# A transformer layer with a product-key expert stage: a wider dense part of V in rounded halves, and sixteen dots on TensorE

## The chip, the cores and the metric

The kernel runs on one core of one Trainium2 chip. The metric is the device time of one execution in microseconds; a core's engines are TensorE (PE), VectorE (DVE), ScalarE (ACT), GpSimd (POOL) and SyncE (SP), which run their own instruction streams and meet through semaphores. Sixteen DMA engines move data between HBM and the on-chip memory (SBUF).

## The reference

One layer on 256 tokens of width 2048: a mixer (two kinds of attention) and then an expert stage. Only the expert stage is touched:

```python
def chunk(xc):                                   # 128 tokens
    qc = (xc @ w_query).reshape(C, 8, 2, 128)
    s = einsum('chpd,hpnd->chpn', qc, sub_keys)  # 2 x 128 keys a head
    top_s, top_i = lax.top_k(s, 16)
    ...                                          # 16 of the 256 sums, an expert of 16384 each
    g = softmax(best_s)
    act = gelu(einsum('chkd,cd->chk', expert_u[expert_idx], xc))
    return einsum('chk,chkd->cd', g * act, expert_v[expert_idx])
x = x + out
```

Each token picks 8 x 16 = 128 experts, so each of the two tiles of 128 tokens has 128 picks: for pick m a row of `expert_u` (2048 floats) is fetched for each token and its dot product with the token is taken, and the row of `expert_v` is added with the weight that follows from it.

## The kernel before

The work of the two tiles is numbered as 256 picks, m = 0 to 255; 16 picks are a "head" here, heads 0 to 7 belong to tile 0 and 8 to 15 to tile 1. Partition p holds token p of a tile.

**U stage.** POOL issues one indirect DMA per pick (line 691, 128 rows of 8 KB, 1 MiB) into one of eight places (`ring`; six from pick `U_WIDE` on). DVE takes the dot in one pass over the row (`pick_dot_of`, line 1549) and raises `dotted`; between the dots it does the top-k work of the next head (`head_part`, ten parts in the first ten picks of a head), and the last part gives `pick_row`, without which POOL can't issue the next head's gathers. From m = 112 (`V_FROM`) on POOL puts a gather of V between every four of U (`v_gather`, line 671); V rows are only `V_ROW` = 1152 wide. The first 36 of them (`V_BESIDE`) are added by PE: ACT makes a diagonal matrix of the weights (line 917) and PE multiplies it with the rows (`pick_add`, line 2095, true fp32).

**Dense part.** The other `V_DENSE` = 896 columns of V aren't gathered. For each token a 128 x 128 matrix of its weights over all 16384 experts is built from two one-hot matrices (`group`, line 2118, four tokens each), and moved by ACT into `dense_w[t][b, a, token]` (`group_out`, line 961). Then PE multiplies it, block a of 128 expert rows by block, with the whole table: `dense(a)`, line 2127, 128 blocks, both tiles, fp32. The blocks are loaded by SP into four places (line 598), each as soon as the block four before it has been used.

**Seam.** Tile 0's weights are built beside the U stage; tile 1's, which need the last dot, in the stage between it and the first dense block, called the seam. `SEAM` is the order of the V rows there: DVE adds one after two of every three groups of four tokens (line 1597), PE one after every second group; 37 rows in all, into seven places. Per group DVE makes two one-hot blocks (line 1582), ACT scales four matrices and moves the result, PE multiplies four pairs.

**Tail.** PE runs the 128 dense blocks; DVE adds the 183 rows of V that are left, POOL gathers them through the seven places in order. The last row's add is cut in two, and the outputs leave by DMA.

Of the kernel before, what the change touches and what calls it, by code (L numbers as in the profile page):

```python
# [14 lines left out]
P = 128  # L15
# [118 lines left out]
U_WIDE = 108  # L134
# [3 lines left out]
V_ROW = 1152  # L138
V_DENSE = D - V_ROW
V_FROM, V_BESIDE = 112, 36  # L140
# [9 lines left out]
SEAM = sorted([(i, "dve", i) for i in range(GROUPS) if i % 3] + [(i + 2, "pe", i) for i in range(GROUPS) if i % 2])  # L150
# [3 lines left out]
DENSE_AT = (4 * 512, 6 * 512)  # L154

# [17 lines left out]

def v_place(k):

    return k % V_FIRST_PLACES if k < V_BESIDE else (k - V_BESIDE) % V_PLACES
# [12 lines left out]
def v_until(m):  # L189

    return max(0, m - V_FROM + 1) // 4
# [43 lines left out]
def layer(nc, x, norm1_g, w_in, cmp_pe, cmp_k_w1, cmp_k_w2, cmp_v_w1, cmp_v_w2, q_norm_g, k_norm_g,  # L235
          rel_bias_table, sb_out_g, nsa_out_g, w_out, norm2_g, peer_w_query, peer_sub_keys,
          peer_expert_u, peer_expert_v, onehot, out):
    with ExitStack() as ctx:
# [147 lines left out]
        assert A_XN <= at_big[0] - DENSE_PLACES * V_DENSE and at_big[0] <= A_X1T  # L386
        hot0 = ring_rest.rearrange("p (s j n) -> p s j n", s=2, j=GROUP_TOKENS)
# [26 lines left out]
        query_used = sem("query_used")  # L414

# [195 lines left out]
        def _(pool):  # L611
# [63 lines left out]
            for m in range(PICKS):  # L675
                if m in (0, 8):
                    pool.wait_ge(sem("first_rows"), m // 8 + 1)
                elif m % TOPK == 0:
                    pool.wait_ge(head_step, (m // TOPK + 1) * HEAD_OPS)
                if m == 0:  # L680
                    pool.wait_ge(split_free, SP_END + SPLIT)
                if m == EARLY - 1:
                    pool.wait_ge(sem("rows_gained"), TT * W_CHUNKS)
                if m == TOPK - 4:
                    power(8, rstd[:, 1:2])
                f = before_in_place(m)
                if f >= 0:
                    pool.wait_ge(dotted, f + 1)
# [11 lines left out]
        def _(act):  # L700
# [233 lines left out]
            def hot_first(i):  # L934

                for j in range(GROUP_TOKENS):
# [4 lines left out]
                    act.activation(v, iota[:, :], ACT.Square, bias=picks_t[:, 1, token:token + 1], scale=-1.0).then_inc(sem("hot_squared"), 1)  # L941
                    act.wait_ge(sem("hot_squared"), token + 1)
# [15 lines left out]
            def group_out(t, i):  # L958

                act.wait_ge(token_made, t * P + (i + 1) * GROUP_TOKENS)  # L960
                act.activation(dense_w[t][:, :, i * GROUP_TOKENS:(i + 1) * GROUP_TOKENS],
                               ps[:, 3 + i % 2, :].rearrange("p (j a) -> p a j", j=GROUP_TOKENS), ACT.Copy).then_inc(group_moved, 1)

            for m in range(PICKS):
# [7 lines left out]
                if k == 1 and n:  # L972
                    head_gelu(n - 1)
                if m == TURN_0 + 1:
# [3 lines left out]
                    act.wait_ge(sem("picks_here"), 2)  # L978
                i = group_at(m)
# [9 lines left out]
                for p in v_at(m):  # L989
                    pick_diag(p)  # L990
# [11 lines left out]
            act.wait_ge(sem("out_ready"), 1)  # L1002
            act.wait_ge(added, dve_adds(TILE_PICKS))
            act.dma_start(out_rows[:, 0, 0:V_ROW], X[:, 0, 0:V_ROW]).then_inc(out_stored, 16)
            act.wait_ge(dense_used, NKEYS)
            v = slice(V_ROW, V_ROW + CHUNK)
            act.activation(X[:, 1, v], ps[:, 6, :], ACT.Copy).then_inc(sem("dense_copied"), 1)  # L1007
            act.wait_ge(sem("dense_copied"), 1)
# [4 lines left out]
        def _(dve):  # L1013
# [537 lines left out]

            def head_weights(n):
                v = slice(n * TOPK, (n + 1) * TOPK)
                dve.wait_ge(sem("head_acted"), n + 1)
                dve.wait_ge(sem("exp_inverse"), n + 1)
# [101 lines left out]
            for k in range(V_AFTER, PICKS):  # L1657
                if k == V_AFTER + V_PLACES:
# [10 lines left out]
        def _(pe):  # L1669
# [416 lines left out]
            def pick_add(k):  # L2086

                row = v_here(pe, k)
                if k == 0:
                    pe.wait_ge(sem("pq_first"), 3)  # L2090
# [5 lines left out]
                ins.then_inc(pe_added, 1)  # L2096

# [8 lines left out]
            def group(t, i):  # L2106

                if t * GROUPS + i >= 2:
# [5 lines left out]
                for j in range(GROUP_TOKENS):  # L2114
# [3 lines left out]
                    pe.matmul(ps[:, 3 + i % 2, j * P:(j + 1) * P], hot[:, 1, :], hot[:, 0, :], start=True, stop=True).then_inc(token_made, 1)  # L2118

            def dense(a):  # L2120

                pe.wait_ge(dense_loaded[a % DENSE_PLACES], 16 * (a // DENSE_PLACES + 1))
# [33 lines left out]
            for m in range(PICKS):  # L2156
# [5 lines left out]
                if k == TOPK - 1 and n + 2 < HEADS:  # L2162
# [5 lines left out]
                if i is not None:  # L2168
                    group(0, i)
                if m == TURN_1:  # L2170
                    pe.wait_ge(head_step, HEADS * HEAD_OPS)
                    turn_picks(1, (0, 1))
                for p in v_at(m):
                    pick_add(p)
            pe.wait_ge(sem("head_weighted"), HEADS)
# [37 lines left out]
```

## Time and profile before

| | |
|---|---|
| median of 3 runs | 1690.85 us (1689.32 to 1690.89) |
| the profiled execution | 1694.34 us, its span 1692.5 us |
| granted TensorE clock, mean | 0.843 of full |
| busy: PE, DVE, ACT, POOL | 73%, 77%, 27%, 50% of the span |
| moved by DMA | 575.81 MB, 340 GB/s over the span |

Times below are from the start of the span. A clock of 1.0 is 2.4 GHz and 0.5 is 1.2 GHz. An fp32 matmul of the program leaves two records in the profile, and one dot of line 1549 two as well (the pass, and the read of its accumulator). Records of pipelined instructions overlap, so the distance between two starts is the cost of one, and the mean duration is more. The stages: dots from 463 to 1201, the seam from 1201 to 1280, dense blocks from 1280 to 1666, and the end at 1692.5.

### The profile page before, as it was taken

The numbers are of one execution on the slowest core, as the hardware profiler recorded it, in microseconds if no ns is written. First come the engines' busy times: TensorE is split into PE (matmuls) and PEld (weight loads), VectorE is DVE, ScalarE is ACT, GpSimd is POOL, SyncE is SP. The second block draws the span as 40 slices with busy tenths as digits, with TensorE's granted clock in tenths as the row PEclk, the third lists the DMA queues.
The fourth block names the chain that finished last, engine by engine and source line by source line (L and its number), as shares of the span: only waits on it lengthen the run. The fifth ranks groups of instructions, "written<-read, shape, count | busy, mean of one in ns | idle before, by whom it ended". The sixth has DMA issues, their size and how long they took to land.

```text
span 1692.5 us, 14464 instructions
## 1 busy us (share of the span) xinstructions
PE 1234.9 (73%) x4812; PEld 839.8 (50%) x4812; DVE 1298.5 (77%) x1802; ACT 460.9 (27%) x1023; POOL 842.8 (50%) x546
## 2 busy tenths in 40 slices
PE   9999999999995554001344544454699999999993
PEld 7888887778984343000122322332365555555551
DVE  5554666466699999999999999999796665666667
ACT  5333443554200100000135565552381000000000
POOL 1000010000174888877888888888565443444444
PEclk9999999999997778555666676666699999999997
DMA  8886546348799999999999999999899999999998
GB/s 237 223 207 196 169 143 213 99 148 278 260 410 415 422 411 396 385 371 362 395 382 407 403 413 387 398 401 422 335 313 380 410 409 411 410 410 409 410 409 347
DMA packets 150230, 575.81 MB, mean 340 GB/s; under 512 B 15586, under 2 KB 28596, under 8 KB 117268
## 3 DMA queue, kind: packets, MB, share of 16 engines
q0 software_dynamic: 74384, 421.30, 62.6%
q1 hardware_dynamic: 75460, 152.82, 26.9%
q8 instruction: 35, 0.57, 0.1%
q10 hardware_dynamic: 320, 0.86, 0.1%
q14 instruction: 31, 0.25, 0.0%
HBM read 572.57 MB, written 2.36 MB: 340 GB/s over the span
## 4 chain that ended last, share of the span: by engine, by line
PE 30%; DVE 28%; DMA 24%; POOL 12%; issue 4%; ACT 2%; DVEq 0%; ACTq 0%; POOLq 0%
DMA v_rows<-in_peer_expert_v,pick_row 21%; DVE big L1549 10%; DVE more_rows L1549 8%; PE ps L1692 6%; PE ps L1694 6%; PE ps L1693 6%; POOL big L691 5%; PE ps L2095 4%; POOL more_rows L691 3%; DVE big L1597 3%; POOL v_rows L671 3%; DMA more_rows<-in_peer_expert_u,pick_row 2%; PE ps L2118 1%; DMA big<-in_peer_expert_u,pick_row 1%; DVE big L1574 1%
## 5 line engine op out<-in xcount | busy, mean ns | idle before, releaser
L671 POOL DMA_INDIRECT v_rows<-in_peer_expert_v,pick_row x256 | 307.8, 1202 | 271.7 <-DVE big L1597 234.9
L1597 DVE SCALAR_TENSOR_TENSOR big<-v_rows,pick_w,big 128x1152 f32<-128x1152 f32 x203 | 287.6, 1417 | 151.7 <-DMA v_rows<-in_peer_expert_v,pick_row 149.7
L2095 PE MATMUL ps<-v_rows,diag 128*128 128x512 f32 (+1 forms) x312 | 182.9, 746 | 269.5 <-DMA v_rows<-in_peer_expert_v,pick_row 169.8
L1549 DVE CUSTOM_DVE_ANT_0 big<-big 128x2048 f32<-128x2048 f32 x150 | 340.1, 2283 | 12.9 <-DMA big<-in_peer_expert_u,pick_row 12.5
L691 POOL DMA_INDIRECT big<-in_peer_expert_u,pick_row x150 | 288.8, 1925 | 65.6 <-issue 43.2
L2095 PEld LDWEIGHTS ps<-v_rows,diag 128*128 128x128 f32 x312 | 83.3, 285 | 368.2 <-issue 194.8
L691 POOL DMA_INDIRECT more_rows<-in_peer_expert_u,pick_row x106 | 222.7, 2101 | 75.3 <-issue 28.3
L1030 DVE TENSOR_TENSOR split_lo<-raw,split_hi 128x1024 fp32r<-128x1024 f32 x119 | 145.8, 1225 | 143.7 <-ACT split_hi L719 118.1
L1549 DVE CUSTOM_DVE_ANT_0 more_rows<-more_rows,big 128x2048 f32<-128x2048 f32 x106 | 240.8, 2284 | 11.0 <-DMA more_rows<-in_peer_expert_u,pick_row 11.0
L2127 PE MATMUL ps<-big,dense 128*128 128x512 f32 (+1 forms) x512 | 213.5, 539 | 0.3 <-DMA big<-in_peer_expert_v 0.3
L2127 PE MATMUL ps<-big 128*128 128x512 f32 (+1 forms) x512 | 213.4, 539 | 0.0
L1692 PE MATMUL ps<-split_hi,ht 128*128 128x512 f32 x476 | 189.3, 398 | 1.1 <-DVE split_lo L1080 0.9
L1694 PE MATMUL ps<-split_hi,ht 128*128 128x512 f32 x476 | 185.9, 390 | 0.0
L1693 PE MATMUL ps<-split_lo,ht 128*128 128x512 f32 x476 | 185.7, 390 | 0.0
L634 POOL TENSOR_TENSOR small<-small 128x2 f32<-128x2 f32 (+4 forms) x8 | 12.7, 1592 | 329.3 <-DVE small L1228 95.4
L2127 PEld LDWEIGHTS ps<-big,dense 128*128 128x128 f32 x512 | 97.1, 190 | 95.7 <-issue 61.2
L2127 PEld LDWEIGHTS ps<-big 128*128 128x128 f32 x512 | 97.3, 190 | 95.1 <-issue 61.2
L719 ACT ACTIVATE split_hi<-raw 128x1024 fp32r<-128x1024 f32 x97 | 102.9, 1060 | 148.9 <-PE ps L1694 148.1
L2118 PE MATMUL ps<-big 128*128 128x128 f32 x512 | 83.8, 324 | 50.5 <-ACT big L948 49.6
L1007 ACT ACTIVATE big<-ps 128x512 f32<-128x512 f32 x1 | 0.6, 598 | 388.0 <-PE ps L2127 388.0
L2118 PEld LDWEIGHTS ps<-big 128*128 128x128 f32 x512 | 78.5, 238 | 53.8 <-issue 50.9
L1692 PEld LDWEIGHTS ps<-split_hi,ht 128*128 128x128 f32 x476 | 89.4, 188 | 27.6 <-issue 3.2
(281 smaller groups left out, 1495.2 us busy)
## 6 DMA issues: line engine op xcount, KB each, us to landing
big<-in_peer_expert_v SPq DMA_DIRECT2D x128, 448.0 KB, 6.8
raw<-in_w_in SPq DMA_DIRECT2D x88, 512.0 KB, 3.7
raw<-in_w_out SPq DMA_DIRECT2D x32, 512.0 KB, 5.1
big<-in_peer_w_query SPq DMA_DIRECT2D x16, 512.0 KB, 6.5
raw<-in_peer_w_query SPq DMA_DIRECT2D x8, 512.0 KB, 7.6
spare<-in_peer_w_query SPq DMA_DIRECT2D x8, 512.0 KB, 8.3
v_rows<-in_peer_expert_v,pick_row POOLq DMA_INDIRECT x256, 14.2
big<-in_peer_expert_u,pick_row POOLq DMA_INDIRECT x150, 9.1
```

The costliest lines, as they stand in the source:

```text
L671: pool.indirect_dma_start(v_row(k), None, v_table, bass.IndirectOffsetOnAxis(pick_row[:, k:k + 1], 0)).then_inc(v_gathered[v_place(k)], 16)
L691: pool.indirect_dma_start(ring[u_place(m)], None, u_table, bass.IndirectOffsetOnAxis(pick_row[:, m:m + 1], 0)).then_inc(gathered[u_place(m ...
L719: act.activation(split_hi[:, s % SPLIT, :], raw[:, s % RAW, :], ACT.Copy).then_inc(hi_done, 1)
L1030: dve.tensor_tensor(split_lo[:, slot % SPLIT, 0:width], raw[:, slot, 0:width], split_hi[:, slot % SPLIT, 0:width].bitcast(F32), ALU.subtra ...
L1549: dve.tensor_tensor_reduce(row, row, XN[:, place_of(m // TOPK)[0], :], 1.0, 0.0, ALU.mult, ALU.add, pick_dot[:, m:m + 1]).then_inc(dotted, 1)
L1597: dve.scalar_tensor_tensor(out=v, in0=row, scalar=pick_w[:, k:k + 1], in1=v, op0=ALU.mult, op1=ALU.add).then_inc(added, 1)
L1692: pe.matmul(acc[t], h_h, w_h, start=k == 0, stop=False)
L1693: pe.matmul(acc[t], h_h, w_l, start=False, stop=False)
L1694: ins = pe.matmul(acc[t], h_l, w_h, start=False, stop=k == KC - 1)
L2095: ins = pe.matmul(psf[:, c:c + w], diag[:, j % DIAGS, :], row[:, c:c + w], start=k == 0, stop=j == pe_adds(PICKS) - 1)
L2118: pe.matmul(ps[:, 3 + i % 2, j * P:(j + 1) * P], hot[:, 1, :], hot[:, 0, :], start=True, stop=True).then_inc(token_made, 1)
L2127: ins = pe.matmul(psf[:, o:o + w], dense_w[t][:, a, :], row[:, c:c + w], start=a == 0, stop=a == NKEYS - 1, skip_group_check=True)
```

## The change

1. Two picks of each of heads 1 to 8 (`TURNED_DOTS`, k = 4 and 10: sixteen dots, m = 20 to 138) are taken by PE: it transposes the row in four groups of four 128 x 128 pieces, ACT copies each group from PSUM into `diag`'s space, PE multiplies it with the token matrix `x1t`, and DVE reads the diagonal of the 128 x 128 product four picks later (`take_dot`). A row's place is free when its last transpose is done.
2. `V_DENSE` grows from 896 to 992, `V_ROW` shrinks from 1152 to 1056.
3. Of the dense blocks, every odd one from 5 on (62 of 128) is split: ACT rounds the V block and the two weight blocks to fp32r (`dense_hi`, `split_w`), DVE subtracts to get the rest (`split_low`), and PE does three fp32r passes (high x high, high x low, low x high) in place of one fp32 product. The order of `split_low` among DVE's V adds is fixed: the one of block a stands where the share (a-2)/128 of the tail's V adds is done.
4. V gathers beside U begin at m = 144, one to three of U, 37 in all, and `U_WIDE` is 138. In the seam DVE adds a row after every group, and three rows are added by PE ahead of the first group: 50 rows. 169 are left for the tail, in five places, since `dense_hi` takes the room.
5. `head_scores` of a later head moves from k = 15 to k = 13 (9 for tile 1); diagonals are made ahead of a group's work; the first output's DMA is issued after split block 63.

```diff
-U_WIDE = 108
+U_WIDE = 138
-V_ROW = 1152
+V_ROW = 1056
-V_FROM, V_BESIDE = 112, 36
+V_FROM, V_BESIDE = 144, 37
-SEAM = sorted([(i, "dve", i) for i in range(GROUPS) if i % 3] + [(i + 2, "pe", i) for i in range(GROUPS) if i % 2])
+SEAM_FIRST = 3
+SEAM = sorted([(-1, "pe", i - SEAM_FIRST) for i in range(SEAM_FIRST)] + [(i, "dve", i) for i in range(1, GROUPS)] + [(i + 2, "pe", i) for i in range(GROUPS) if i % 2])
+HI_PLACES, HI_BEHIND = 2, 4
+V_LATE = 5
+SPLIT_BLOCKS = [a for a in range(HI_BEHIND, NKEYS) if a % 2]
+SPLIT_AHEAD = 2
...
 def v_until(m):
 
-    return max(0, m - V_FROM + 1) // 4
+    return max(0, m - V_FROM + 1) // 3
...
+            for r, a in enumerate(SPLIT_BLOCKS):
+                act.wait_ge(dense_loaded[a % DENSE_PLACES], 16 * (a // DENSE_PLACES + 1))
+                act.wait_ge(dense_used, a - HI_BEHIND + 1)
+                act.activation(dense_hi[:, r % HI_PLACES, :], dense_rows[:, a % DENSE_PLACES, :], ACT.Copy).then_inc(dense_high, 1)
+                for t in range(TT):
+                    ins = act.activation(split_w[t][:, a - HI_BEHIND, :], dense_w[t][:, a, :], ACT.Copy)
+                ins.then_inc(dense_high, 1)
...
+            def split_low(a):
+
+                r = SPLIT_BLOCKS.index(a)
+                dve.wait_ge(dense_high, 2 * r + 1)
+                dve.tensor_tensor(dense_lo[:, a % DENSE_PLACES, :], dense_rows[:, a % DENSE_PLACES, :],
+                                  dense_hi[:, r % HI_PLACES, :].bitcast(F32), ALU.subtract).then_inc(dense_split, 1)
+                dve.wait_ge(dense_high, 2 * r + 2)
+                for t in range(TT):
+                    ins = dve.tensor_tensor(split_w[t][:, a, :], dense_w[t][:, a, :], split_w[t][:, a - HI_BEHIND, :].bitcast(F32), ALU.subtract)
+                ins.then_inc(dense_split, 1)
+
...
+            def turned_dot(m):
+
+                q, t = TURNED_DOTS.index(m), place_of(m // TOPK)[0]
+                row = row_here(pe, m)
+                if q == 0:
+                    pe.wait_ge(sem("pq_first"), 3)
+
+                def turn(c):
+                    g = q * DOT_GROUPS + c
+                    if g >= 2:
+                        pe.wait_ge(turned_here, g - 1)
+                    for j in range(KC // DOT_GROUPS):
+                        k = c * DOT_GROUPS + j
+                        ins = pe.transpose(ps[:, g % 2, j * P:(j + 1) * P], row[:, k * P:(k + 1) * P], ident[:, :])
+                    ins.then_inc(row_turned, 1)
+
+                def add(c):
+                    if c == 0 and q >= 2:
+                        pe.wait_ge(dotted, dots_until(TURNED_DOTS[q - 2]))
+                    pe.wait_ge(turned_here, q * DOT_GROUPS + c + 1)
+                    for j in range(KC // DOT_GROUPS):
+                        k = c * DOT_GROUPS + j
+                        ins = pe.matmul(ps[:, 2 + q % 2, 0:P], turned_rows[:, j, :], x1t[:, k, t * P:(t + 1) * P], start=k == 0, stop=k == KC - 1)
+                    ins.then_inc(turned_used, 1)
...
+                if a in SPLIT_BLOCKS:
+                    r = SPLIT_BLOCKS.index(a)
+                    pe.wait_ge(dense_split, 2 * r + 2)
+                    hi, low = dense_hi[:, r % HI_PLACES, :], dense_lo[:, a % DENSE_PLACES, :]
+                    for t in range(TT):
+                        w_hi, w_low = split_w[t][:, a - HI_BEHIND, :], split_w[t][:, a, :]
+                        for w, row in ((w_hi, hi), (w_hi, low), (w_low, hi)):
+                            for c in range(0, V_DENSE, CHUNK):
+                                o, n = DENSE_AT[t] + c, min(CHUNK, V_DENSE - c)
+                                last = a == NKEYS - 1 and w is w_low
...
```

How the rows stand on the engines, at three places. First DVE in the seam: line 1582 (1649 after) makes the one-hot blocks of a group of four tokens, line 1597 (1664 after) adds a V row. Before:

```order
L1582 TENSOR_TENSOR big<-iota,picks_t 128x512 x2
L1597 SCALAR_TENSOR_TENSOR big<-v_rows,pick_w,big 128x1152
L1582 TENSOR_TENSOR big<-iota,picks_t 128x512 x4
L1597 SCALAR_TENSOR_TENSOR big<-v_rows,pick_w,big 128x1152
L1582 TENSOR_TENSOR big<-iota,picks_t 128x512 x2
```

After, at the same place:

```order
L1649 TENSOR_TENSOR big<-iota,picks_t 128x512 x2
L1664 SCALAR_TENSOR_TENSOR big<-v_rows,pick_w,big 128x1056
L1649 TENSOR_TENSOR big<-iota,picks_t 128x512 x2
L1664 SCALAR_TENSOR_TENSOR big<-v_rows,pick_w,big 128x1056
L1649 TENSOR_TENSOR big<-iota,picks_t 128x512 x2
```

Three groups had two adds between them, now they have three.

Second, DVE in the tail, where before 175 adds of line 1597 stand in a row behind the sum of tile 0 (line 1604). After, from the last group of the seam on (line 1731 is the split of a V block, line 1735 that of a weight block):

```order
L1649 TENSOR_TENSOR big<-iota,picks_t 128x512 x2
L1664 SCALAR_TENSOR_TENSOR big<-v_rows,pick_w,big 128x1056 x4
L1731 TENSOR_TENSOR dense_lo<-big,dense_hi 128x992
L1735 TENSOR_TENSOR split_w_53<-dense_51,split_w_53 128x128
L1735 TENSOR_TENSOR split_w_54<-big,split_w_54 128x128
L1664 SCALAR_TENSOR_TENSOR big<-v_rows,pick_w,big 128x1056 x3
L1731 TENSOR_TENSOR dense_lo<-big,dense_hi 128x992
L1735 TENSOR_TENSOR split_w_53<-dense_51,split_w_53 128x128
L1735 TENSOR_TENSOR split_w_54<-big,split_w_54 128x128
```

Behind every two or three adds DVE now has three subtractions, which wait for ACT and the block's load, and the adds behind them wait with them.

Third, PE in the tail. Before, each block is these four products (the first two for tile 0, whose weights are `dense_51` in the rows; the others for tile 1):

```order
L2127 MATMUL ps<-big,dense_51 128x512
L2127 MATMUL ps<-big,dense_51 128x384
L2127 MATMUL ps<-big 128x512
L2127 MATMUL ps<-big 128x384
```

After, an even block has four such of line 2256 (512 and 480 wide), and an odd one, here its half for tile 0, stands behind it as:

```order
L2256 MATMUL ps<-big 128x512
L2256 MATMUL ps<-big 128x480
L2248 MATMUL ps<-dense_hi,split_w_53 128x512
L2248 MATMUL ps<-dense_hi,split_w_53 128x480
L2248 MATMUL ps<-dense_lo,split_w_53 128x512
L2248 MATMUL ps<-dense_lo,split_w_53 128x480
L2248 MATMUL ps<-dense_hi,split_w_53 128x512
L2248 MATMUL ps<-dense_hi,split_w_53 128x480
```

An odd block went from four fp32 products to twelve fp32r ones.

## Rows read from the trace of the kernel before

**Rows 1.** The page, part 2: the span in 40 slices.

```profile
DMA  8886546348799999999999999999899999999998
```

**Rows 2.** Stages by windows of all engines (us, busy us and instructions).

```profile
core 0: us, PE busy (x) PEld busy (x) DVE busy (x) ACT busy (x) POOL busy (x), PEclk, DMA share, GB/s
602.00:775.40 173.40, 37.05 (x118) 28.72 (x116) 172.24 (x279) 14.12 (x21) 133.71 (x64) 0.62 0.96 383
775.40:870.80 95.40, 31.29 (x61) 14.88 (x61) 88.07 (x143) 16.07 (x44) 83.51 (x40) 0.61 0.98 393
870.80:1200.90 330.10, 160.46 (x439) 96.32 (x440) 313.97 (x479) 157.05 (x455) 283.55 (x139) 0.64 1.00 403
1200.90:1280.00 79.10, 71.62 (x359) 50.44 (x358) 70.87 (x90) 60.01 (x178) 47.35 (x41) 0.90 0.88 306
1280.00:1666.40 386.40, 386.13 (x1028) 194.68 (x1026) 237.75 (x169) 0.00 (x0) 162.89 (x170) 1.00 1.03 409
```

**Rows 3.** DVE around two dots, from the timeline of 1000 to 1012.

```profile
1003.76 2.28 DVE L1549 CUSTOM_DVE_ANT_0 more_rows<-more_rows,big 128x2048 f32<-128x2048 f32 x1
1005.97 2.28 DVE L1549 CUSTOM_DVE_ANT_0 big<-big 128x2048 f32<-128x2048 f32 x1
```

**Rows 4.** POOL in the same stretch, and once in the tail, from the timeline.

```profile
1000.49 0.94 POOL L691 DMA_INDIRECT big<-in_peer_expert_u,pick_row  x1 [1.67 <-DVE pick_dot L1549]
1001.74 2.91 POOL L671 DMA_INDIRECT v_rows<-in_peer_expert_v,pick_row  x1 [0.30 <-issue]
1004.95 1.91 POOL L691 DMA_INDIRECT more_rows<-in_peer_expert_u,pick_row  x1 [0.30 <-issue]
...
1401.16 0.94 POOL L671 DMA_INDIRECT v_rows<-in_peer_expert_v,pick_row  x1 [1.53 <-DVE big L1597]
```

**Rows 5.** DVE in the seam, from the timeline of 1244 to 1251.

```profile
1244.65 1.28 DVE L1582 TENSOR_TENSOR big<-iota,picks_t 128x512 f32<-128x512 f32 x2
1245.86 1.40 DVE L1597 SCALAR_TENSOR_TENSOR big<-v_rows,pick_w,big 128x1152 f32<-128x1152 f32 x1
1247.19 2.52 DVE L1582 TENSOR_TENSOR big<-iota,picks_t 128x512 f32<-128x512 f32 x4
```

**Rows 6.** PE in the seam, and the seam's one long wait of DVE.

```profile
1244.91 2.18 PE L2095 MATMUL ps<-v_rows,diag 128*128 128x512 f32 x6 [0.17 <-ACT diag L917]
1249.04 2.18 PE L2095 MATMUL ps<-v_rows,diag 128*128 128x512 f32 x6 [0.17 <-ACT diag L917]
...
1223.19 1.29 DVE L1582 TENSOR_TENSOR big<-iota,picks_t 128x512 f32<-128x512 f32 x2 [6.09 <-PE ps L2118]
```

**Rows 7.** Groups of instructions in the tail, 1280 to 1692.5, shapes apart.

```profile
L1597 DVE SCALAR_TENSOR_TENSOR big<-v_rows,pick_w,big 128x1152 f32<-128x1152 f32 x180 | 255.3, 1418 | 149.9 <-DMA v_rows<-in_peer_expert_v,pick_row 148.1
L1665 DVE TENSOR_TENSOR big<-big,ps 128x896 f32<-128x896 f32 x1 | 1.1, 1078 | 0.0
```

**Rows 8.** PE in the tail: two half-blocks' records, from the timeline.

```profile
1400.17 1.67 PE L2127 MATMUL ps<-big 128*128 128x512 f32 x4
1401.68 1.67 PE L2127 MATMUL ps<-big,dense 128*128 128x512 f32 x4
```

**Rows 9.** PE in the first projection, fp32r products, from the timeline.

```profile
150.66 0.39 PE L1692 MATMUL ps<-split_hi,ht 128*128 128x512 f32 x1
151.34 0.39 PE L1692 MATMUL ps<-split_hi,ht 128*128 128x512 f32 x1
```

**Rows 10.** The page, part 5: the splits of the projections' weights.

```profile
L1030 DVE TENSOR_TENSOR split_lo<-raw,split_hi 128x1024 fp32r<-128x1024 f32 x119 | 145.8, 1225 | 143.7 <-ACT split_hi L719 118.1
L719 ACT ACTIVATE split_hi<-raw 128x1024 fp32r<-128x1024 f32 x97 | 102.9, 1060 | 148.9 <-PE ps L1694 148.1
```

**Rows 11.** The dense loads of line 598.

```profile
DMA to landing us min/median/max: 3.6/6.8/10.8
```

**Rows 12.** The end, from the timeline.

```profile
1661.68 24.25 DVE L1597 SCALAR_TENSOR_TENSOR big<-v_rows,pick_w,big 128x1152 f32<-128x1152 f32 x16 [0.57 <-DMA v_rows<-in_peer_expert_v,pick_row]
...
1686.03 1.54 DVE L1593 SCALAR_TENSOR_TENSOR big<-v_rows,pick_w,big 128x576 f32<-128x576 f32 x2
```

More of the change, by code:

```diff
@@ L154, with split_after @@
 DENSE_AT = (4 * 512, 6 * 512)
+HI_PLACES, HI_BEHIND = 2, 4
+V_LATE = 5
+SPLIT_BLOCKS = [a for a in range(HI_BEHIND, NKEYS) if a % 2]
+SPLIT_AHEAD = 2
+OUT_0_AT = 63
+def split_after(n):
+    return [a for a in SPLIT_BLOCKS if max(0, a - SPLIT_AHEAD) * (PICKS - V_AFTER) // NKEYS == n]
 def u_place(m):
@@ L960, in group_out, with turned_copies @@
                 act.wait_ge(token_made, t * P + (i + 1) * GROUP_TOKENS)
+                if t == 0 and i == 0:
+                    act.wait_ge(turned_used, ALL_TURNED)
                 act.activation(dense_w[t][:, :, i * GROUP_TOKENS:(i + 1) * GROUP_TOKENS],
-                               ps[:, 3 + i % 2, :].rearrange("p (j a) -> p a j", j=GROUP_TOKENS), ACT.Copy).then_inc(group_moved, 1)
+                               ps[:, 4 - i % 2, :].rearrange("p (j a) -> p a j", j=GROUP_TOKENS), ACT.Copy).then_inc(group_moved, 1)
+            def turned_copies(q):
+                for g in range(q * DOT_GROUPS, (q + 1) * DOT_GROUPS):
+                    act.wait_ge(row_turned, g + 1)
+                    if g:
+                        act.wait_ge(turned_used, g)
+                    act.activation(turned_rows.rearrange("p c n -> p (c n)"), ps[:, g % 2, :], ACT.Copy).then_inc(turned_here, 1)
             for m in range(PICKS):
@@ L978, in _ @@
                     act.wait_ge(sem("picks_here"), 2)
+                for p in v_at(m):
+                    pick_diag(p)
                 i = group_at(m)
@@ L988, in _ @@
                     picks_here(1, 1)
-                for p in v_at(m):
-                    pick_diag(p)
+            for i in range(-SEAM_FIRST, 0):
+                pick_diag(SEAM_V["pe", i])
             head_gelu(HEADS - 1)
@@ L1550, in pick_dot_of, with take_dot @@
                                          pick_dot[:, m:m + 1]).then_inc(dotted, 1)
+            def take_dot(m):
+                q = TURNED_DOTS.index(m)
+                dve.wait_ge(turned_used, DOT_GROUPS * (q + 1))
+                dots = ps[:, 2 + q % 2, 0:P]
+                dve.tensor_tensor_reduce(dots, dots, ident[:, :], 1.0, 0.0, ALU.mult, ALU.add, pick_dot[:, m:m + 1]).then_inc(dotted, 1)
             def head_weights(n):
@@ L2096, in pick_add @@
                 ins.then_inc(pe_added, 1)
+            def turned_dot(m):
[19 more added lines that the diff above has]
+                    ins.then_inc(turned_used, 1)
+                turn(0)
+                for c in range(1, DOT_GROUPS):
+                    turn(c)
+                    add(c - 1)
+                add(DOT_GROUPS - 1)
             def turn_picks(t, parts):
@@ L2106, in group @@
             def group(t, i):
+                if t == 0 and i == 1:
+                    pe.wait_ge(dotted, dots_until(TURNED_DOTS[-1]))
                 if t * GROUPS + i >= 2:
@@ L2161, in _ @@
                     queries(*QUERY_MADE[m])
-                if k == TOPK - 1 and n + 2 < HEADS:
+                if k == SCORES_AT[n // NH] and n + 2 < HEADS:
                     head_scores(n + 2)
@@ L2174, in _ @@
                     pick_add(p)
+            for i in range(-SEAM_FIRST, 0):
+                pick_add(SEAM_V["pe", i])
             pe.wait_ge(sem("head_weighted"), HEADS)
```

69 lines of the change are left out of this document (52 added, 17 removed).

## The prediction

> **What bounds the kernel now.** I read the DMA line over the span first, then windows of all engines by stage, then for each stage the engine that has no idle time. The DMA line [rows 1] stands at 9 from the first dots to the end, but for one slice near 750 us and two in the seam. So bytes matter, but the stages differ [rows 2]:
>
> - *Heads 3 to 6 (602 to 775.4), U rows only.* 43.35 us a head. VectorE is busy 172.24 of 173.4 us, the DMA share is 0.96 at 383 GB/s. VectorE bounds it: a dot costs 2.21 us, the distance of two starts [rows 3], 16 make 35.4, and the rest is top-k work of the next head.
> - *Heads 7 and 8 (775.4 to 870.8)*, the first with V rows between: 47.7 us a head.
> - *Heads 9 to 15 (870.8 to 1200.9).* 47.2 us a head, share 1.00, 403 GB/s. VectorE is busy 95% and GpSimd, with 139 gathers of 2.04 us and 0.30 us between them [rows 4], 325 of 330. Three limits lie together.
> - *The seam.* DMA 0.88 only. VectorE and TensorE are nearly full.
> - *The tail (1280 on).* TensorE has 386.13 of 386.4 us, the DMA 1.03 at 409 GB/s. TensorE ends at 1666.4; the last V rows, 16 adds in 24.25 us [rows 12], end 20 us later. So DMA ends last and TensorE is close behind.
>
> **The change part by part.**
>
> *A. Sixteen dots leave VectorE, V starts at 144.* Per head it loses two dots (4.42 us) and gets two short reads of a PSUM diagonal. No row shows that read; it lies between nothing and the 0.61 us of a 128x512 operation (half of the 1.21 us between the pair and the add, [rows 5]); I take 0.3. VectorE then needs 39.5 us a head. DMA takes over: a head's U rows are 16.78 MB, at 403 GB/s 41.6 us (41.0 at the tail's 409, 42.7 at 393). Since V rows are gone from heads 7 and 8, all six heads go at that: 250 against 173.4 + 95.4 = 268.8 us, **-19** (-23 to -13). TensorE's part of a dot is covered: it is busy 37 of 173 us there, and VectorE asks for the result four picks later, 10.4 us after the row lands. If a dot takes more than that, VectorE stands before the top-k parts and GpSimd behind it. Heads 1 and 2 share the DMA with query weights and I cost them at nothing.
>
> *B. 37 V rows beside seven heads.* A head has 16.78 MB of U and 5.33 V rows of 0.541 MB, 19.66 MB: 48.8 us at 403 GB/s, 341.5 against 330.1, **+11**. Lower bound: at 409 GB/s, +6.5. Upper bound by GpSimd: 21.33 gathers of 330.1/140 = 2.36 us are 50.3 us a head, +22. I take the DMA's, because a gather falls to 0.94 us when VectorE waits [rows 4], and VectorE will wait where DMA is late.
>
> One rule of the Trainium skill bears on this (SBUF — State Buffer, "Who interferes with whom"): an operation of VectorE with two SBUF inputs takes only the read side of the port pair that it shares with GpSimd, and writing descriptors needs the write side. By it a gather costs the same beside a dot, GpSimd would be half idle in B, and the upper bound of +22 would go. The trace disagrees: 1.91 and 2.91 us beside dots, 0.94 in gaps [rows 4].
>
> *C. Seam.* A group costs VectorE 1.21 us of one-hots, an add 1.33 [rows 5]; three groups with two adds are 6.29 us, 2.10 a group. TensorE needs 4.13 us for two groups [rows 6], 2.07 each. Now every group has an add of 1056: 1.33 x 1056/1152 = 1.22, so 2.43 us a group; VectorE alone bounds. 30 groups: +9.9. At the seam's start three V adds go ahead of the first group. Their rows can't be gathered before the add of row 36 frees its place, and TensorE has rested, at about half clock. In exchange the wait of 6.09 us [rows 6], for a group behind late V rows, shrinks. Net I take +1.5 (-3 to +6). **+11** in all (+7 to +16).
>
> *D. Tail.* Before it is 412.5 us. After:
> - TensorE: half a block is 1.51 us [rows 8], a block 3.01; 992 wide 3.33. An fp32r product of 512 costs (151.34 - 150.66)/3 = 0.227 us [rows 9], one of 480 0.213; twelve are 2.64. 66 x 3.33 + 62 x 2.64 = 383.5 us. The extra width eats the passes saved.
> - DMA: 128 blocks of 0.508 MB and 169 rows of 0.541 are 156.4 MB, at 409 GB/s 382 us; before 166.7 MB and 407.
> - VectorE: 169 adds of 1.42 x 1056/1152 = 1.30 [rows 7], 62 splits of 1.225 x 992/1024 = 1.19 [rows 10] and about 0.5 for two weight blocks (each less than the 0.61 of a 512-wide one): 325 us. Not the bound.
> - The chain of a split block: block a-4 used, load, ACT's copy 1.03 (1.06 x 992/1024, [rows 10]), VectorE 1.7, handoffs about 0.3. With the load at its median of 6.8 us [rows 11] that is 9.8 us. TensorE covers it with a-3 to a-1: 3.33 + 2.64 + 3.33 = 9.3. So 0.5 us short in each four blocks, 16 us over 32 of them; but the load took 3.6 us at best, and with five places for V rows in place of seven less is pending beside it. I take half, 8 us.
> - End: from the last adds at 1686.03 [rows 12] it is 6.5 us to the end; I keep that behind the last block.
>
> 383.5 + 8 + 6.5 = 398: **-14.5**. Bounds: -22.5 without any stall; the other end is the first rival.
>
> The Trainium skill has a rule on the load (DMA: Bandwidth & Descriptors, "Queues, rings and completion order"): each DMA engine takes the queues that have work in turn, a packet from each. So a block's load pays for V rows beside it, and it speaks against this change, since a split block has no time for that. By the rule alone the load stays at 6.8 while V is pending, and D would be -6.5, the total 1688; the row's 3.6 to 6.8 is why I take less.
>
> *Sum.* -19.2 + 11.4 + 11.4 - 14.5 = -10.9. The span goes from 1692.5 to 1681.6; the profiled execution was 1.84 above its span (1694.34) and 3.49 above the median, so the median is **1680 us**.
>
> **The rivals.**
>
> *R1, slower: the split blocks come late (0.13).* If VectorE is in an add (1.3 us) or waits for a V row when the block is ready, the chain is 11.1, and four blocks take 11.1 + 2.64 = 13.75 us in place of 11.94: 440 us, the tail 446, the total 1728. With half the delay, 13.1 us, 1707. For: the order on VectorE is fixed, and the adds behind a split wait with it. Against: late blocks thin the V traffic, and loads get faster. It decides at four blocks in 12.6 us: above that the whole gain is gone.
>
> *R2, no change or slower: GpSimd is the limit of the U stage (0.12).* If gathers stay tied to VectorE's passes, B is +22 and A only -13: the U stage loses 9 instead of gaining 8, total about 1696. For: its idle time there is all "issue" of 0.30. Against: fewer passes are what frees it.
>
> *R3, better all over (0.18).* VectorE relieved, U rows at 409 GB/s (A -23, B +6.5), no stall in the tail (-22.5), seam +9: -30, 1661.
>
> *R4, the dots on TensorE give nothing (0.07)*, because VectorE stands for their results: A then keeps only V's removal, 6 x 43.35 = 260, -9: 1690.
>
> **How the numbers follow.** My forecast has 0.50, its own range 1670 to 1687. The range with R3's and R2's nearer halves is 1664 to 1697. A measurement tells 0.2%, 3.4 us, from no change. Faster by more (below 1687.5): forecast, R3, and a little of R4, 0.71. Within it: R4 and part of R2, 0.13. Slower: R1 and most of R2, 0.16.
>
> **What would show it.** Dots 48 to 143 in 250 us with VectorE idle before U rows and the DMA share at 1.0 (A). Seven heads in 340 us; over 350 with GpSimd never waiting is R2. Adds and one-hots back to back in the seam at 2.4 us a group (C). In the tail TensorE's waits for the split of line 1731 or 1735: 8 us in sum; four blocks in 12.2 us. If those waits are over 25 us, D is wrong and R1 right; if DMA falls below 0.95 there, the five places are too few. The likeliest error is D's stall, a small difference of two large numbers.

## The result: slower by 0.3 to 0.9%

The changed kernel takes 1702.14 us (median of 10 runs, 1698.56 to 1714.73), the kernel before 1691.95 us in the same set. The ratio is 1.0075, 95% interval 1.0058 to 1.0093. In a second set of the same kernel (run e10) the ratio was 1.0045 (1.0032 to 1.0058). The forecast was 1680 us, and faster.

The profiled execution is the longest of the ten, 1714.73 us with a span of 1712.5; that of e10, 1696.64 us with a span of 1694.4, is shorter than its median of 1699.53. I use both, since what they share is the kernel's; numbers in brackets are e10's. By windows of all engines, with the columns of [rows 2], first the changed kernel:

```profile
602.00:775.00 173.00, 92.36 (x517) 80.18 (x518) 168.93 (x304) 34.31 (x55) 141.53 (x69) 0.76 1.01 420
775.00:870.00 95.00, 47.04 (x233) 36.18 (x233) 94.00 (x165) 35.64 (x89) 74.72 (x38) 0.73 0.99 395
870.00:1189.00 319.00, 176.06 (x453) 100.70 (x451) 287.94 (x422) 148.16 (x425) 267.51 (x135) 0.66 0.98 392
1189.10:1283.40 94.30, 71.67 (x372) 49.60 (x372) 77.88 (x99) 60.49 (x178) 64.16 (x50) 0.96 0.85 295
1283.40:1706.00 422.60, 399.09 (x1276) 237.44 (x1275) 315.21 (x356) 89.18 (x187) 235.49 (x169) 1.00 0.98 370
```

And the seam and the tail of the same kernel in e10:

```profile
1181.90:1271.50 89.60, 73.00 (x372) 50.17 (x372) 77.30 (x97) 61.98 (x178) 59.42 (x50) 0.94 0.89 310
1271.50:1688.00 416.50, 397.73 (x1276) 236.13 (x1275) 314.89 (x356) 89.39 (x187) 235.80 (x169) 1.00 0.99 376
```

The DMA's share over 40 slices of the changed kernel:

```profile
DMA  8886556258799999999999999998889999999998
```

Between the dots' start and the last slice it has three slices below 9, all around the seam (1156 to 1284 us); [rows 1] has a single one, 1185 to 1227 us.

Against [rows 2]: GpSimd has issued 69 gathers from 602 to 775 in place of 64 to 775.4, at 420 GB/s in place of 383. The last dot ends at 1189.1 (e10: 1181.9) in place of 1200.9. The seam takes 94.3 (89.6) us for 79.1. The tail, from the first dense block to the end of the span, takes 429.1 (422.9) us for 412.5. So the U stage gave 12 (19) us, the seam took 15 (10), and the tail, where the change was to win 14.5, lost 17 (10).

In the tail before, TensorE was busy 386.13 of 386.4 us and the DMA was at 1.03 and 409 GB/s. Now TensorE has holes of 23 (19) us, and the DMA moves only 370 (376) GB/s at a share of 0.98 (0.99). The waits of the changed kernel there (engine, line, releaser: us, times, longest):

```profile
ACT dense_hi L1059 <- DMA big<-in_peer_expert_v: 330.0, 62, 17.3
DVE dense_lo L1731 <- ACT dense_hi L1059: 66.3, 43, 4.3
PEld ps L2248 <- DVE split_w L1735: 57.3, 55, 3.4
DVE big L1664 <- DMA v_rows<-in_peer_expert_v,pick_row: 34.7, 22, 10.7
PE ps L2248 <- DVE split_w L1735: 22.0, 29, 2.7
```

ScalarE waits for the load before each of the 62 splits, VectorE for ScalarE, TensorE's split blocks for VectorE's last subtraction. One split block of the changed kernel from its load's issue on, from the timelines of SP, ACT, DVE and PE:

```profile
1403.59 0.33 SPq L632 DMA_DIRECT2D big<-in_peer_expert_v  x1
...
1410.73 1.03 ACT L1059 ACTIVATE dense_hi<-big 128x992 fp32r<-128x992 f32 x1 [4.32 <-DMA big<-in_peer_expert_v]
...
1411.80 1.27 DVE L1731 TENSOR_TENSOR dense_lo<-big,dense_hi 128x992 fp32r<-128x992 f32 x1 [0.23 <-ACT dense_hi L1059]
...
1413.19 0.28 DVE L1735 TENSOR_TENSOR split_w<-big,split_w 128x128 fp32r<-128x128 f32 x1
...
1413.85 0.77 PE L2248 MATMUL ps<-dense_hi,split_w 128*128 128x512 f32 x1
```

From the load's issue to ScalarE's start it is 7.14 us, and 10.26 to TensorE. All loads of the changed kernel took:

```profile
DMA to landing us min/median/max: 4.1/7.1/8.6
```

before, the median was 6.8 [rows 11]. Over all 62 blocks the medians are 7.15 us to ScalarE, 1.03 its copy, 0.03 to VectorE, 1.60 its three subtractions, 0.06 to TensorE: 9.9 us. Then come the block's own passes, 2.8 us (1400.59 to 1403.40, below), and only then may the load of the block four later be issued, 0.19 us behind them. In the timeline of PE, the split block four before the one above (1400.59), whose place its load took at 1403.59, and the split block between the two (1408.11), for which TensorE waited 1.23 us:

```profile
1400.59 0.71 PE L2248 MATMUL ps<-dense_hi,split_w 128*128 128x512 f32 x2 [0.26 <-DVE split_w L1735]
...
1403.40 1.82 PE L2256 MATMUL ps<-big,dense 128*128 128x512 f32 x4
...
1408.11 0.73 PE L2248 MATMUL ps<-dense_hi,split_w 128*128 128x512 f32 x2 [1.23 <-DVE split_w L1735]
```

The loop of four blocks is thus 12.9 us by its medians, and by means, where the late ones count, 13.1: 10.05 from the load's issue to TensorE and 3.08 from there to the next load's issue (e10: 9.89 and 3.05). Such a sum would close in any kernel with these places; what shows that the chain sets the pace is that TensorE starts 0.06 us after the last subtraction at the median; where it has other work to do, as in e8 below, it comes 2.1 us later. By starts of TensorE, blocks 8 to 124, four blocks take 13.14 us (12.94 in e10), before 12.03.

### The profile page after: what moved, and what is told of

Its sections match the earlier page's. It is cut to its first block, busy times and chain, and to the rows that moved or that the text cites. A ratio compares the mean times of both kernels' runs of the same rounds, so it can differ in the third digit from the quotient of the medians.

```text
span 1712.5 us, 17141 instructions
## 1 busy us (share of the span) xinstructions
PE 1347.2 (79%) x5852; PEld 972.8 (57%) x5852; DVE 1336.8 (78%) x1984; ACT 590.4 (34%) x1277; POOL 914.9 (53%) x546
## 4 chain that ended last, share of the span: by engine, by line
PE 32%; POOL 25%; DMA 20%; DVE 13%; issue 7%; ACT 2%; DVEq 0%; ACTq 0%; POOLq 0%
POOL big L727 12%; DMA big<-in_peer_expert_v 8%; DMA big<-in_peer_expert_u,pick_row 7%; POOL more_rows L727 7%; PE ps L1775 6%; PE ps L1777 6%; PE ps L1776 6%; DMA v_rows<-in_peer_expert_v,pick_row 5%; POOL v_rows L705 5%; PE ps L2248 5%; DVE more_rows L1610 4%; DVE big L1664 2%; PE ps L2256 2%; DVE big L1610 1%; ACT dense_hi L1059 1%
## 5 line engine op out<-in xcount | busy, mean ns | idle before, releaser
L705 POOL DMA_INDIRECT v_rows<-in_peer_expert_v,pick_row x256 | 366.3, 1431 | 233.5 <-DVE big L1664 159.1
L1664 DVE SCALAR_TENSOR_TENSOR big<-v_rows,pick_w,big 128x1056 f32<-128x1056 f32 x199 | 261.8, 1316 | 54.0 <-DMA v_rows<-in_peer_expert_v,pick_row 44.8
L2178 PE MATMUL ps<-v_rows,diag 128*128 128x512 f32 x336 | 181.9, 698 | 150.8 <-DMA v_rows<-in_peer_expert_v,pick_row 149.1
L1059 ACT ACTIVATE dense_hi<-big 128x992 fp32r<-128x992 f32 x62 | 63.9, 1030 | 330.0 <-DMA big<-in_peer_expert_v 330.0
L2248 PE MATMUL ps<-dense_hi,split_w 128*128 128x512 f32 x496 | 153.0, 410 | 22.2 <-DVE split_w L1735 22.0
L2194 PE MATMUL ps<-ident,big 128*128 128x128 f32 x240 | 47.3, 348 | 112.2 <-DMA big<-in_peer_expert_u,pick_row 112.2
L2248 PEld LDWEIGHTS ps<-dense_hi,split_w 128*128 128x128 f32 x496 | 90.1, 189 | 76.1 <-DVE split_w L1735 57.3
L1731 DVE TENSOR_TENSOR dense_lo<-big,dense_hi 128x992 fp32r<-128x992 f32 x62 | 74.0, 1194 | 66.5 <-ACT dense_hi L1059 66.3
L2256 PE MATMUL ps<-big,dense 128*128 128x512 f32 (+1 forms) x264 | 121.0, 581 | 0.0
L2256 PE MATMUL ps<-big 128*128 128x512 f32 (+1 forms) x264 | 120.6, 579 | 0.0
```

The lines of the kernel that those rows point to most:

```text
L705: pool.indirect_dma_start(v_row(k), None, v_table, bass.IndirectOffsetOnAxis(pick_row[:, k:k + 1], 0)).then_inc(v_gathered[v_place(k)], 16)
L1664: dve.scalar_tensor_tensor(out=v, in0=row, scalar=pick_w[:, k:k + 1], in1=v, op0=ALU.mult, op1=ALU.add).then_inc(added, 1)
L2178: ins = pe.matmul(psf[:, c:c + w], diag[:, j % DIAGS, :], row[:, c:c + w], start=k == 0, stop=j == pe_adds(PICKS) - 1)
L2248: ins = pe.matmul(psf[:, o:o + n], w, row[:, c:c + n], start=False, stop=last, skip_group_check=True)
L2256: ins = pe.matmul(psf[:, o:o + w], dense_w[t][:, a, :], row[:, c:c + w], start=a == 0, stop=a == NKEYS - 1, skip_group_check=True)
```

## The experiments

Theory T1: that loop sets the tail, and TensorE's and the DMA's work don't. Rivals: T2, the DMA does, slowed by the new row sizes (3968 and 4224 bytes for 3584 and 4608); T3, VectorE or the five V places do; T4, the loss is from the U stage or the seam. Each ratio is to the kernel before in the same set of runs.

**e1, weights first.** ScalarE and VectorE treat the weight blocks while the load is under way:

```diff
+                act.wait_ge(dense_used, a - HI_BEHIND + 1)
+                for t in range(TT):
+                    ins = act.activation(split_w[t][:, a - HI_BEHIND, :], dense_w[t][:, a, :], ACT.Copy)
+                ins.then_inc(dense_high, 1)
                 act.wait_ge(dense_loaded[a % DENSE_PLACES], 16 * (a // DENSE_PLACES + 1))
-                act.wait_ge(dense_used, a - HI_BEHIND + 1)
                 act.activation(dense_hi[:, r % HI_PLACES, :], dense_rows[:, a % DENSE_PLACES, :], ACT.Copy).then_inc(dense_high, 1)
-                for t in range(TT):
-                    ins = act.activation(split_w[t][:, a - HI_BEHIND, :], dense_w[t][:, a, :], ACT.Copy)
-                ins.then_inc(dense_high, 1)
```

and the same swap in `split_low`. 

> The changed kernel, but the weight blocks of a split block are rounded and subtracted while its load is still under way, so only the V block's own copy and subtraction stand between landing and the three passes. Theory T1 (the chain of a split block, load 7.1 + copy 1.03 + subtractions 1.60 + the block's own passes 2.81 us, sets the pace of four blocks, 13.1 us): the chain loses the two weight subtractions, 0.4 us, so 12.7 us and 13 us less over 32 cycles, about 1689 us, ratio about 0.999. Rival T2 (the DMA sets the tail, slowed by packets of 3968 and 4224 bytes): no change, 1702 us, ratio 1.0075. Rival T3 (VectorE or the five V places set it): no change either.

Measured: 1693.81 us, ratio 1.0007 (0.9993 to 1.0021), 0.4 to 0.7% less than the change. Four blocks take 12.77 us. A reordering that changes neither bytes nor work moved the time; T2 falls as the sole cause. The gain is 8 us against the 1702 and 6 against e10's 1699.5, where T1 had 13: four blocks lost 0.17 to 0.37 us, not 0.4.

**e2, TensorE starts early.** On top of e1 the passes of a split block are ordered high x high, low weights x high, high x low, for both tiles each, and wait apart:

```diff
-                    pe.wait_ge(dense_split, 2 * r + 2)
...
+                    for which in range(3):
+                        if which == 0:
+                            pe.wait_ge(dense_high, 2 * r + 2)
+                        else:
+                            pe.wait_ge(dense_split, 2 * r + which)
```

> As the kernel with the weights first, and TensorE starts a split block with high x high as soon as ScalarE has rounded it, then low weights x high, then high x low: VectorE's subtraction is hidden behind 1.9 us of passes. T1: the chain falls to load 7.1 + copy 1.03 + handoffs 0.2 = 8.3 us, under the 9.5 of the three other blocks, so TensorE itself bounds: 12.3 us for four blocks, 27 us less, about 1676 us, ratio about 0.99. T2: still 1.0075. T3: small gain at most, 1.005.

Measured: 1673.17 us, ratio 0.9892 (0.9876 to 0.9908), T1's 0.99. The timeline of one split block of e2 shows why: TensorE begins 0.2 us after VectorE has begun the subtraction for which it waited before, and doesn't stop.

```profile
1402.43 1.19 DVE L1735 TENSOR_TENSOR dense_lo<-big,dense_hi 128x992 fp32r<-128x992 f32 x1
1402.62 2.35 PE L2252 MATMUL ps<-dense_hi,split_w 128*128 128x512 f32 x8
1404.81 1.06 PE L2252 MATMUL ps<-dense_lo,split_w 128*128 128x512 f32 x4
```

Its dense stage by windows: TensorE full, the DMA back at 1.01 and 400 GB/s.

```profile
1276.50:1668.00 391.50, 389.17 (x1277) 239.82 (x1275) 312.65 (x355) 89.44 (x187) 213.31 (x169) 1.00 1.01 400
```

**e3, the old tail.** U stage and seam of the change; 896 columns dense, no block split, V rows 1152 wide in seven places.

```diff
-V_ROW = 1056
+V_ROW = 1152
-V_LATE = 5
-SPLIT_BLOCKS = [a for a in range(HI_BEHIND, NKEYS) if a % 2]
+V_LATE = 7
+SPLIT_BLOCKS = []
```

> The U stage and the seam of the change (sixteen dots by TensorE, V from pick 144, 50 rows in the seam) with the dense part as before: 896 wide, all blocks true fp32, V rows 1152 wide in seven places. T1: dense blocks start at about 1283 to 1287 and take 386 us; the V rows left are 169 of 0.590 MB beside 58.7 MB, 158.5 MB or 387 us; end about 1680 us, ratio 0.993. If the loss came from the U stage or the seam instead (T4), this kernel is at 1700 us or above, ratio over 1.003.

Measured: 1679.75 us, ratio 0.9939 (0.9916 to 0.9963). So T4 falls: with the old tail the rest of the change gains 0.6%, and the new tail costs 1.1 to 1.4%. The gain doesn't lie in the two stages themselves, whose first dense block starts at 1279.0 us for 1280.0 before; it lies behind TensorE's last block, since 14 V rows fewer are left for the tail: 12 us from the last block to the end, where it was 26.

```profile
1279.00:1666.00 387.00, 385.90 (x1028) 194.78 (x1026) 235.25 (x166) 0.60 (x1) 168.12 (x169) 1.00 1.02 408
```

**e4, 992 columns without splits.** As e3, but `V_ROW` stays 1056.

> The changed kernel with 992 columns dense but every block in true fp32, V rows in seven places. TensorE needs 128 blocks of 3.33 us = 426 us without any wait, so the tail is 433 against 429 in the profiled run and 417 in the median one: about 1716 us, ratio 1.015. T2 (DMA-bound tail): the same bytes, so the same time as the change, 1.0075.

Measured: 1710.99 us, ratio 1.0111 (1.0093 to 1.013), less than the 1.015 expected. With the same bytes as the change it is 9 us slower, and TensorE has 426.94 of 427.2 us:

```profile
1278.80:1706.00 427.20, 426.94 (x1029) 194.86 (x1027) 224.62 (x172) 0.22 (x1) 168.17 (x169) 1.00 0.92 367
```

TensorE needs 40 us more than the splits' own work (387 us, e8 below); in the change 28 to 34 us of these come back as waiting, since its dense stage, from first block to last, is 415 to 421 us.

**e5, all dots on VectorE.** As e3, with an empty `TURNED_DOTS` and without the waits on it.

```diff
-TURNED_DOTS = [n * TOPK + k for n in range(1, NH + 1) for k in (4, 10)]
+TURNED_DOTS = []
```

> The kernel with the old tail (896 wide, no splits), and all 256 dots back on VectorE; V still from pick 144 and 50 rows in the seam. If the dots on TensorE are what speeds heads 3 to 8, those six heads go back to 43.35 us each, 260 us, where the changed kernel's U gathers 48 to 144 took 244: 16 us more, about 1696 us, ratio 1.003. If the later start of V gave the gain and the dots nothing (the prediction's fourth rival), it stays at 1680 us, ratio 0.994.

Measured: 1700.54 us, ratio 1.0057 (1.0036 to 1.0078), 21 us over e3, where 16 were expected. By windows from 602 to 775.4 VectorE is full again as before, and the DMA at 0.96:

```profile
602.00:775.40 173.40, 37.01 (x118) 28.62 (x116) 172.71 (x277) 13.97 (x21) 139.57 (x65) 0.62 0.96 389
```

Between the issue of gathers 48 and 144 it needs 262.3 us, e3 243.3. The sixteen dots are worth 19 us there; the prediction's R4 falls.

**e6, the old seam** on e2: `SEAM` as before, 37 rows in the seam, 182 in the tail.

> The kernel in which TensorE starts a split block early, with the seam of before (VectorE adds a row after two of three groups, none ahead): 37 rows in the seam, 182 left for the tail. The seam gets shorter by 11 us (VectorE 2.10 us a group for 2.43). The tail has 13 rows more, 163.4 MB or 400 us at 409 GB/s, where TensorE needs 391: plus 9 us. So about the same, 1671 us, ratio 0.988. If TensorE alone set the tail, 1662 us, ratio 0.983; if the three rows ahead save a long wait at the seam's start, 1676 us or more.

Measured: 1676.55 us, ratio 0.9891 (0.9859 to 0.9923). The ratio is e2's. The seam went from 89.4 to 74.1 us, 15 less, and the dense stage from 390 to 404, for the rows that it got back:

```profile
1187.20:1261.30 74.10, 67.37 (x353) 47.97 (x354) 65.68 (x89) 60.27 (x178) 46.13 (x38) 0.93 0.81 286
1261.30:1666.00 404.70, 397.20 (x1277) 236.46 (x1275) 326.18 (x367) 89.16 (x187) 216.00 (x181) 1.00 1.01 402
```

Where V rows stand is nearly neutral: a row costs about as much in the seam as in the tail.

**e7, half the splits**: the changed kernel with `if a % 4 == 1` in `SPLIT_BLOCKS`, and the first output's DMA behind block 61.

> The changed kernel with half the splits: 31 blocks (5, 9, 13, ...) in three passes, 97 in true fp32. By TensorE's work alone it should be slower than the change: 97 x 3.33 + 31 x 2.81 = 410 us against 394. T1 (the chain of load 7.1, copy 1.0, subtractions 1.6 and the own passes 2.8, 12.7 us, is longer than four blocks' work): now four blocks have 12.8 us of work, the chain is just covered, the tail is 410 to 413 us in place of 417, about 1697 us, ratio 1.002. If the stalls came from something that doesn't hang on the splits (DMA rate, V places), it is 16 us slower than the change: 1718 us, ratio 1.015.

Measured: 1697.87 us, ratio 1.004 (1.0017 to 1.0063). Undoing half of the splits adds about 20 us of work to TensorE (31 blocks of 3.34 us, by e4, in place of 2.68, by e8), and the kernel doesn't get slower; by the medians it is 4 us faster than the change, but its interval overlaps with both of the change's. In the dense stage TensorE is busy 409.85 us of 413.20; in the change it was 399 of 422.6.

```profile
1274.10:1687.30 413.20, 409.85 (x1153) 216.17 (x1151) 269.55 (x263) 44.29 (x93) 219.60 (x169) 1.00 0.99 379
```

**e8, narrow V rows in the tail.** The rows of the tail are gathered 128 of 1056 wide, and every instruction stays; most of the tail's V product is left out.

```diff
-                pool.indirect_dma_start(v_row(k), None, v_table,
+                pool.indirect_dma_start(v_row(k)[:, 0:128] if k >= V_AFTER else v_row(k), None, v_table,
```

> The changed kernel, but the 169 V rows of the tail are gathered only 128 of 1056 wide (what stands in the places from earlier rows is added for the rest, so this leaves out most of the tail's V traffic; every instruction stays). T1 with the load's length set by the V packets beside it: the load falls from 7.1 to about 4 us, the chain to 9.6, and TensorE bounds the tail with 394 us of work: about 1679 us, ratio 0.992. If the load takes 7 us for another reason, the time stays at 1702, ratio 1.006.

Measured: 1670.77 us, ratio 0.988 (0.9849 to 0.9911). One split block's load and ScalarE's start, from the timelines of e8: 4.03 us, where the change has 7.14; the median of the 62 is 3.93.

```profile
1402.03 0.33 SPq L632 DMA_DIRECT2D big<-in_peer_expert_v  x1
...
1406.06 1.03 ACT L1059 ACTIVATE dense_hi<-big 128x992 fp32r<-128x992 f32 x1 [5.01 <-DMA big<-in_peer_expert_v]
```

The waits of line 2248 for line 1735 are gone, four blocks take 12.03 us, and TensorE is busy in all of its 386.90 us:

```profile
1279.30:1666.20 386.90, 386.90 (x1276) 240.04 (x1275) 316.77 (x357) 88.78 (x186) 242.58 (x169) 1.00 0.62 197
```

The splits, VectorE's order and the five places are the change's, and what makes the chain too long is the V traffic beside the load. Narrow rows also land sooner, so e8 alone would leave room for a VectorE that is late because of its V rows. But it is late by only 0.17 us a split block in the change (mean, from ScalarE's copy to VectorE's start) and 0.07 in e8, 6 us at most over the 62, and e2 runs at full pace with the same five places; so T3 falls.

It isn't the number of V rows that are pending. Counted from issues and landings, 6.3 gathers on average were on their way when a load of the tail was issued before, and 3.5 in the change, and a gather landed after 14.4 us at the median before and after 8.9 in the change. The load beside them took 6.8 us before and 7.1 in the change, with 11% more bytes. That agrees with the Trainium skill (DMA: Bandwidth & Descriptors, "Queues, rings and completion order"), by which each DMA engine takes its queues in turn. How much of the load's time is this turn-taking and how much the plain sharing of a full DMA, no run separates.

**e9, 960 columns dense** on e2 (`V_ROW = 1088`).

> The kernel in which TensorE starts a split block early, with 960 columns dense in place of 992 (V rows 1088 wide). There the tail had TensorE at 389 of 391.5 us and the DMA at 1.01, so the narrower block should cut TensorE's work by 960/992, 12 us, and the bytes rise from 156.4 to 157.0 MB, 384 us at 409 GB/s. The tail is then DMA-bound at about 386 us, 5 less; the U stage and seam cost 1 or 2 us more: about 1669 us, ratio 0.987. If TensorE's stalls and not its work fill the tail, no gain.

Measured: 1678.09 us, ratio 0.9921 (0.9905 to 0.9936), a miss: 0.3% slower than e2's ratio, not 0.2% faster. TensorE is busy 383.12 us, 6 less than in e2 where 12 were foreseen, and the dense stage still takes 391.5:

```profile
1275.00:1666.50 391.50, 383.12 (x1277) 237.24 (x1275) 312.87 (x354) 87.87 (x187) 186.96 (x169) 1.00 1.02 402
```

The DMA moves 402 GB/s, not the 409 that I had put in: at that the 157.0 MB are 390.5 us. Why it is 400 to 402 beside splits (e2, e6, e9) and 408 in e3 wasn't tried; the rows' sizes, T2's reason, aren't excluded for these 2%, which is too little for the loss. The ratios of e9 and e2 are at the edge of what their intervals tell apart.

**e11, none ahead** on e2: the three V rows ahead of the seam's first group are left to the tail.

> The kernel in which TensorE starts a split block early, without the three V rows ahead of the seam's first group (47 rows in the seam, 172 for the tail). The rows ahead delay the first group until their gathers have landed, behind the add of row 36; the seam was 89 to 94 us for 79 before, where the adds by VectorE account for 10. Without them the seam should be 3 to 6 us shorter and the tail about 7 us of DMA longer, of which TensorE's 391 us hide most: 1670 to 1674 us, ratio 0.989. If the rows ahead hide a longer wait, as the old seam's 6 us of VectorE behind TensorE, it is 1677 us or more.

Measured: 1673.22 us, ratio 0.9889 (0.9872 to 0.9906). The seam is 85.4 us, 4 less, the dense stage 2.8 more; no difference in the time.

**e10, the change again.** 

> The changed kernel unaltered, beside the others on one chip, for a second profile of it. 1702 us, ratio 1.006 to 1.008; in its tail four blocks in 13.0 us, the load at 7.1 us.

Measured: 1699.53 us, ratio 1.0045 (1.0032 to 1.0058), a little under the expected range.

## Why the prediction was wrong

*What bounds the kernel before*: held. VectorE set heads 3 to 8 (e5 shows it from the other side), the DMA with TensorE close behind the tail (e3).

The DMA line of [rows 1] was misread in the prediction: it has no slice below 9 near 750 us, and one in the seam.

*A*, -19 forecast: from dot 48 to dot 144 it is 242.4 us (242.5) for 268.8, **-26** (by the issue of gathers, 243.9 for 273.3). The mechanism was right and the size too small, since I took 403 GB/s from heads 9 to 15 and the U rows alone ran at 420. The page of the kernel before had that rate, which I overlooked: 422 GB/s in the fourteenth slice, 550 to 592 us, where U gathers ran alone at a share of 1.01.

```profile
GB/s 237 223 207 196 169 143 213 99 148 278 260 410 415 422 411 396 385 371 362 395 382 407 403 413 387 398 401 422 335 313 380 410 409 411 410 410 409 410 409 347
```

The read of the diagonal took 0.295 us; I had 0.3. Dot 48 comes 3 (5) us earlier than before, in heads whose cost I had put at nothing.

*B*, +11 forecast: from dot 144 to the last it is 347.9 us (342.1) for 330.0, **+18** (+12); gathers 144 to 255 are issued in 343.7 us (340.4) for 328.1. GpSimd has no wait but the 0.30 of issue there, the DMA 0.98 and 392 GB/s (e10: 0.99, 399). What set it, GpSimd or DMA, no run separates. I called the longer gathers beside dots [rows 4] a disagreement of the trace with the rule on the ports; but a gather also reads its row numbers (`pick_row`) from SBUF, so these rows don't tell for which side of the ports it waits.

*C*, +11 forecast: **+15** (e10: +10.5). The steady cost is right: an add every 2.43 us, as 2.43 was worked out, so 9.9 of it. The rest, +5 (+1) for +1.5, is mostly the seam's start: the gather behind row 36 did wait, in the changed kernel 10.95 us, and the first group could start only at 1203.5, 14.4 us after the last dot, where before it was 4.4; against that the wait of 6.09 us [rows 6] shrank to 2.19.

```profile
1188.46 1.50 POOL L705 DMA_INDIRECT v_rows<-in_peer_expert_v,pick_row  x1 [10.95 <-PE ps L2178]
...
1195.07 7.42 PE L2178 MATMUL ps<-v_rows,diag 128*128 128x512 f32 x18 [6.88 <-DMA v_rows<-in_peer_expert_v,pick_row]
...
1203.53 2.44 PE L2234 MATMUL ps<-big 128*128 128x128 f32 x16 [0.89 <-ACT big L993]
```

*D*, -14.5 forecast: **+17** (e10: +10). This is the step that failed: the stall of TensorE behind the split blocks was put at 8 us, and it was 34 (28), the dense stage of 421.3 (415.2) us from first to last block less the 387 that the same work takes in e8. The holes in TensorE's busy time, 23 (19) us, are less than that, since it shows as busy for 399 (398) us with this work. The rest of D was close: TensorE's work 387 us for 383.5, and 7.8 us from the last block to the end for 6.5.

The form of the sum was right. 9.8 us of chain and 2.64 of own passes are 12.44 us, 0.5 more than the 11.94 of four blocks' work, as the prediction had it. Two things went wrong in its sizes. The first is the halving, from 16 us to 8. It rested on a load of 3.6 us and on fewer V rows pending. But the 3.6 us are those of block 0's load, at 1200.9 us, when the DMA stood at 0.68; of the loads of the tail before (1290 to 1650 us) none was near it:

```profile
DMA to landing us min/median/max: 6.6/6.8/8.3
```

And fewer V rows were pending (3.5 for 6.3, above), but the load didn't get shorter by it: 7.1 us. e8 shows that it does fall, to 3.93, when the V bytes are nearly gone. Without the halving the total was 1688, still 14 us short. That is the second: most terms of the loop were sized a little short (means, us).

| term of the loop | forecast | changed kernel | e10 |
|---|---|---|---|
| load's issue to ScalarE's start | 6.8 | 7.10 | 6.97 |
| ScalarE's copy | 1.03 | 1.03 | 1.03 |
| three subtractions | 1.7 | 1.60 | 1.59 |
| handoffs | 0.3 | 0.52 | 0.48 |
| the block's own passes | 2.64 | 2.89 | 2.86 |
| sum | 12.47 | 13.14 | 12.93 |
| work of four blocks | 11.94 | 12.03 | 12.03 |

The stall is the small difference of the last two rows: 1.1 us (0.9) where 0.5 was worked out, and over 31 such loops 34 us (28) in place of 16, or of the 8 that went into the sum.

The sign set for it, TensorE's waits for the split over 25 us, doesn't settle it by its letter: they read 22.0 us on the products and 57.3 on the weight loads, and neither is the stall. The DMA's share stayed at 0.98, and only below 0.95 were the five places to be too few.

*R1* came true in its outcome, near its half size (1707), but not by its mechanism: VectorE was hardly ever late (0.03 us at the median, 0.17 in the mean, between ScalarE's copy and VectorE's start). Its threshold, 12.6 us for four blocks, sorted the kernels rightly: 12.94 and 13.14 are slower than before, e1's 12.77 is level, e2's 12.13 faster. *R2* and *R4* didn't occur; *R3* (1661) wasn't reached even by e2, at 1673, in which the stall is gone.

## What to carry to other kernels

Work that is put between a load and its use on other engines lengthens a loop, not only a busy time: add load, preparation, use and handoffs, and compare the sum with the work of as many blocks as there are places (here four). If the two are close, each small term counts once a loop, so take means and not best cases, and take the load's time from the stage and the traffic that will be beside it. When such a loop is too long, order the use by what is ready first (here, high x high before the rest): that gave 1.5 to 1.8% over the change for no work saved, and made it 1.1% faster than the kernel before.

## What was not expected of the hardware

The same load of 496 KB took 7.1 us beside gathers of 4224-byte rows and 3.9 beside 512-byte ones, with the same number of gathers, and TensorE's tail fell from 421 to 387 us with it. Traffic on another queue, which moves nothing for the block in hand, set its pace, and with 6.3 or 3.5 such gathers pending the load took nearly the same (6.8 us for 448 KB and 7.1 for 496).

U gathers alone ran at 420 GB/s with a share of 1.01, while U and V rows together got 392 to 403 at 0.98 to 1.00, before and after.
